# First block column pair of the conv mixer and of the second feed-forward: seven-product scheme against eight plain block products

## The chip, the cores and the metric

One core of one Trainium2 chip runs the whole program in one launch. The metric is the device time of that core in microseconds (us), median of three runs. TensorE multiplies and sums into PSUM, ScalarE, VectorE and GpSimd work between SBUF and PSUM, and SyncE issues every DMA of the part that matters here.

## The reference, cut to what matters

A step of a two-layer decoder trunk: 1024 prompt tokens and 32 sample tokens, 1056 in all, model width 1024, everything in float32. Layer 0 is sparse attention and a feed-forward, layer 1 a short convolution mixer and a feed-forward. Each sub-layer first normalises its input and scales and shifts it by a condition.

```python
hp = rms_norm(yp, norm1_g[i]) * (1.0 + sc1p) + sh1p
bg, cg, hv = jnp.split(h @ w_in, 3, axis=-1)      # conv mixer, w_in 1024 x 3072
u = cg * hv
y = sum(conv_k[j] * up[:, j:j + T] for j in range(CONV_WIDTH))
return (bg * y) @ w_out
g, u = jnp.split(h @ w_gu, 2, axis=-1)            # feed-forward, w_gu 1024 x 5632
return (jax.nn.silu(g) * u) @ w_down
```

## The kernel before, in words

**Precision.** Each float32 operand is split in two parts, high (a rounded copy, made by ScalarE) and low (the difference, made by VectorE or GpSimd). A product of two blocks is three matmuls: high by high, high by low, low by high.

**Layout.** The result `y` lies in SBUF as eight rows of 128 features by 1056 tokens. The tokens are two groups of 528 (`GS`), a group two halves of 264 (`H`). The three phases behind the attention (`ffn0`, `conv`, `ffn1`, numbered f = 0, 1, 2) share one code. A phase is a list of items (`outline`). A "U" item is one kind of weights (conv: c, h, b; feed-forward: g, u) for a pair of 128-wide output columns. "D" items are the product that comes down again, "P" and "Z" the plain rest of it.

**Seven products.** A U item splits weights (two output columns by two halves of the inner dimension) and tokens (two halves of features by two halves of a group) into 2 x 2 blocks, and gets the four result blocks by seven products in place of eight (Strassen's scheme in Winograd's form). The seven are taken in the order `ORD = (1, 2, 6, 5, 7, 3, 4)`. Products 1, 2 and 3 take token blocks as they are. Products 5, 6, 7 and 4 take sums of token blocks. Of the weights, products 6, 5, 3 and 7 take sums too, made by VectorE (`dve_sums`). A group's token operands are the buffer `th[s]`, with a place `T_AT[i]` for the operand of product i. Results are taken out of PSUM piece by piece by ScalarE (`act_take`) and VectorE (`dve_take`), which add partial results; for kind g a Silu comes on top (`act_silu`).

**First pair of a phase.** Its items are run for one group at a time: kind 1 of group 0, kind 2 of group 0, kind 1 of group 1, kind 2 of group 1. All later ones take both groups at once, 168 matmuls an item. One group takes 84: 7 products, 4 steps of the inner dimension, 3 matmuls. Only the first item of a phase waits for its tokens (`fresh`, in `pe_tokens_ready`), step by step.

**Start of a phase.** While Z runs, ScalarE squares the finished rows, GpSimd adds them (`pool_add`), TensorE sums over the features with a matrix of ones (`pe_sum`), VectorE forms mean and reciprocal, ScalarE the root. Then for group 0, feature tile k by feature tile k (0 to 3), VectorE scales two rows (`dve_scaled`), ScalarE applies scale and shift (`act_affine`), VectorE makes four sums (`dve_t123`, `dve_t4`), ScalarE the high parts (`act_high_b`, `act_high_t`), VectorE the low parts (`dve_low`). The same for group 1 is put between the positions of the first two items (`dve_build`, `act_build`). `pe_sum(f, 1)` stands in TensorE's queue ahead of the first item.

**Weights.** A loaded item lies in one of two raw buffers. Its blocks go one by one through a ring of four, high part by ScalarE (`act_split`), low part mostly by GpSimd (`pool_split`), some by VectorE (`dve_split`). Block n + 4 is prepared at the position of block n. Every engine works its queue in the written order; semaphores tie the queues together.

Of the kernel before, what the change touches and what calls it, by code (L numbers as in the profile page):

```python
# [147 lines left out]
T_AT = {4: 0, 5: 1, 6: 2, 7: 3, 1: 4, 2: 5, 3: 6}  # L148
# [15 lines left out]
def outline(name):  # L164

    kinds, pairs = KINDS[name], N_PAIRS[name]
    for j in range(pairs):
        if j == 0 and name == "conv":
            yield from (("U", k, j, 0, (s,)) for s in BOTH for k in "ch")
            yield "U", "b", j, 0, BOTH  # L170
        elif j == 0:
            yield from (("U", k, j, 0, (s,)) for s in BOTH for k in kinds)
        else:
            yield from (("U", k, j, 0, BOTH) for k in kinds)
# [10 lines left out]
for _f, _name in enumerate(PHASES):  # L185
    for _stage, _kind, _at, _e, _groups in outline(_name):
        _n, _k = len(ITEMS), 7 if _stage in "UD" else 4
        ITEMS.append(Item(_n, _f, _stage, _kind, _at, _e, _groups, len(PREP), None if _stage == "Z" else len(RING), _res))
        for _pos in range(_k):
            if _stage != "Z":  # L190
                SLOT[len(PREP)] = len(RING)
                RING.append(len(PREP))
                DONE.append(_res + (_pos + 1 if _stage == "U" else 2 * _pos + 2 if _stage == "D" else 8 + 8 * (_pos // 2)))
            PREP.append((_n, _pos))
        _res += _k if _stage == "U" else 14 if _stage == "D" else 16
N_RES = _res
IN_PHASE = [[it for it in ITEMS if it.phase == f] for f in range(3)]
U_ITEMS = [[it for it in p if it.stage == "U"] for p in IN_PHASE]
# [6 lines left out]
def units_of(it):  # L205
    return 7 if it.stage in "UD" else 16
# [20 lines left out]
def lo_engine(p):  # L227

    it, pos = ITEMS[PREP[p][0]], PREP[p][1]
    if it.stage != "U":  # L230
        return "pool"
    first = IN_PHASE[it.phase][0].prep
    if p < first + 4:
        return "dve" if it.phase else "pool"
    return "dve" if pos in (1, 6) else "pool"
# [27 lines left out]
for _it in ITEMS:  # L263
    for _u in range(units_of(_it)):
        for _q in range(2 if _it.stage == "D" else 1):
            _set = _par + 2 * _q
            _who = "dve"
            if _it.stage == "U":
# [11 lines left out]
        if _it.stage == "U" and _it.kind in "gc":  # L280
# [4 lines left out]
for _it in ITEMS:  # L285
    if _it.stage == "U" and _it.kind in "ub":
        for _s in _it.groups:
            PAIR_END[_it.phase, _it.at, _s] = TAKEN[_it.res + 6]
PIECE_AT, PIECES_END, _tp = {}, {}, 0
for _a, _b in zip(ITEMS, ITEMS[1:]):  # L290
    if _a.stage == "U" and _a.kind in "ub":
# [32 lines left out]
def lop(g, k, i):  # L324
# [4 lines left out]
    return 20 * g + 5 * k + at + 1  # L329


def program(nc, x_prompt, x_sample, c_prompt, c_sample, cache_k, cache_v, cache_kidx, state_conv, page_table,
# [12 lines left out]
    with ExitStack() as ctx:  # L345
# [43 lines left out]
        (nb0,) = place(AREA["half1"] + 8320, ("nb0", [P, 4, 2, GS], F32))  # L389
# [3 lines left out]
        th = (th0, th1)  # L393
        stages = (stage0, stage1)
# [1893 lines left out]
        def sp_raw(sp, n):  # L2288
# [4 lines left out]
            if n >= 2:  # L2293
                done = ITEMS[n - 2].prep + units_of(ITEMS[n - 2]) - 1 if ITEMS[n - 2].stage in "UD" else ITEMS[n - 2].prep + 3
# [4 lines left out]
            for a in range(2):  # L2299
# [5 lines left out]
                if it.stage == "U":  # L2305
# [47 lines left out]
        def sp_phase(sp, f):  # L2353
            chunks = N_CHUNKS[PHASES[f]]
            for it in U_ITEMS[f]:
# [3 lines left out]
                for k in range(7):  # L2359
# [88 lines left out]
        def pe_u_item(pe, it):  # L2448
            fresh = it.at == 0 and it.kind == FIRST_KIND[it.phase]
            for pos, i in enumerate(ORD):  # L2450
# [3 lines left out]
                for s in it.groups:  # L2454
                    out, x = PS[:, 2 * SET[r] + s, 0:H], th[s][:, :, T_AT[i]]
# [75 lines left out]
        def pe_phase(pe, f):  # L2531
            for it in U_ITEMS[f]:
                if f and it is U_ITEMS[f][0]:
                    pe_sum(pe, f, 1)
                pe_u_item(pe, it)
# [29 lines left out]
        def act_piece(act, n, k):  # L2565
# [6 lines left out]
            act.wait_ge(rd_d, PAIR_END[ph, j, 1 if s is None else s])  # L2572
            after(act, t_st[tp % 2], 16 * (tp // 2))
# [50 lines left out]
        def act_u_item(act, it):  # L2624
            for pos in range(7):
                act_piece(act, it.n, pos)
# [3 lines left out]
                if it.at == 0 and it.groups == (0,):  # L2630
                    act_build(act, it.phase, pos + (7 if it.kind in "uh" else 0))

# [47 lines left out]

        def norm_source(f, s, k, i):
# [24 lines left out]
        def act_z(act, f):  # L2706
# [11 lines left out]
            for i in range(3, 6):  # L2718
                act_square(act, g, 1, i)
            act_affine(act, g, 0, 0)  # L2720
            act_high_b(act, g, 0, 0)
            act_square(act, g, 1, 6)
            act_affine(act, g, 0, 1)
            act_square(act, g, 1, 7)
            act_high_t(act, g, 0, 0)
            act_high_b(act, g, 0, 1)
# [732 lines left out]
```

## Time and profile before

| | us |
|---|---|
| median of 3 runs (2718.96 to 2723.64) | 2723.47 |
| profiled execution | 2723.55 |
| its span, first to last instruction | 2721.7 |
| TensorE busy | 2515.4 (92%) |
| VectorE busy | 1866.8 (69%) |
| ScalarE busy | 1156.2 (42%) |
| GpSimd busy | 1298.9 (48%) |
| mean granted TensorE clock | 0.963 |

Times in the rows are counted from the first instruction. The phase `conv` begins where the Z item of `ffn0` ends, at 1552 us, the phase `ffn1` at 1954 us. TensorE's share is a mean: it is near full within a phase and falls at the starts of phases.

### The profile page before, as it was taken

The numbers are of one execution on the slowest core, as the hardware profiler recorded it, in microseconds if no ns is written. First come the engines' busy times: TensorE is split into PE (matmuls) and PEld (weight loads), VectorE is DVE, ScalarE is ACT, GpSimd is POOL, SyncE is SP. The second block draws the span as 40 slices with busy tenths as digits, with TensorE's granted clock in tenths as the row PEclk, the third lists the DMA queues.
The fourth block names the chain that finished last, engine by engine and source line by source line (L and its number), as shares of the span: only waits on it lengthen the run. The fifth ranks groups of instructions, "written<-read, shape, count | busy, mean of one in ns | idle before, by whom it ended". The sixth has DMA issues, their size and how long they took to land.

```text
span 2721.7 us, 51667 instructions
## 1 busy us (share of the span) xinstructions
PE 2515.4 (92%) x19876; PEld 2309.1 (85%) x19876; DVE 1866.8 (69%) x3356; ACT 1156.2 (42%) x2216; POOL 1298.9 (48%) x988
## 2 busy tenths in 40 slices
PE   6979989999977999999999769999779999999999
PEld 4848864677876999999999769999669999999999
DVE  6488888664269665656667797766796657556675
ACT  4156646774245444444222453332364444442223
POOL 3404642442144656656544435445336566565444
PEclk7999999999997999999999979999889999999999
DMA  8305566103332434444974213328224344359741
GB/s 313 85 17 169 172 225 223 39 1 107 101 96 79 151 127 159 134 143 158 360 294 172 92 52 119 103 87 323 84 59 155 121 159 147 120 183 365 284 152 68
DMA packets 316391, 407.99 MB, mean 150 GB/s; under 512 B 40816, under 2 KB 227032, under 8 KB 313338
## 3 DMA queue, kind: packets, MB, share of 16 engines
q1 hardware_dynamic: 316154, 404.75, 44.3%
q8 instruction: 159, 2.61, 0.4%
q14 instruction: 78, 0.64, 0.1%
HBM read 284.85 MB, written 119.85 MB: 149 GB/s over the span
## 4 chain that ended last, share of the span: by engine, by line
PE 67%; DVE 16%; issue 6%; DMA 5%; POOL 3%; ACT 2%; SPq 1%; DVEq 0%; ACTq 0%; POOLq 0%
PE PS L2460 10%; PE PS L2462 10%; PE PS L2461 10%; PE PS L572 9%; PE PS L2482 5%; PE PS L2484 4%; PE PS L2485 4%; PE PS L1818 2%; PE PS L1847 2%; PE PS L1829 2%; DVE th L2783 1%; DVE s_all L1515 1%; DVE tA L2877 1%; DVE y L2881 1%; POOL ring L2755 1%
## 5 line engine op out<-in xcount | busy, mean ns | idle before, releaser
L2460 PE MATMUL PS<-th,ring 128*128 128x264 f32 x3136 | 911.2, 291 | 79.0 <-DVE y L2914 31.7
L2462 PE MATMUL PS<-th,ring 128*128 128x264 f32 x3136 | 903.7, 288 | 0.0
L2461 PE MATMUL PS<-th,ring 128*128 128x264 f32 x3136 | 902.9, 288 | 0.0
L2460 PEld LDWEIGHTS PS<-th,ring 128*128 128x128 f32 x3136 | 602.4, 192 | 93.1 <-issue 79.4
L2461 PEld LDWEIGHTS PS<-th,ring 128*128 128x128 f32 x3136 | 603.0, 192 | 0.3
L2462 PEld LDWEIGHTS PS<-th,ring 128*128 128x128 f32 x3136 | 603.0, 192 | 0.0
L2755 POOL TENSOR_TENSOR ring<-sums,ring 128x512 fp32r<-128x512 f32 x248 | 363.9, 1469 | 339.1 <-ACT ring L2563 338.8
L2755 POOL TENSOR_TENSOR ring<-wraw,ring 128x512 fp32r<-128x512 f32 x215 | 305.7, 1423 | 370.7 <-ACT ring L2563 370.1
L2482 PE MATMUL PS<-th,ring 128*128 128x264 f32 x1232 | 354.5, 288 | 15.0 <-DVE zs L2973 5.1
L2484 PE MATMUL PS<-th,ring 128*128 128x264 f32 x1232 | 353.1, 287 | 0.0
L2485 PE MATMUL PS<-th,ring 128*128 128x264 f32 x1232 | 352.6, 286 | 0.0
L2970 DVE SCALAR_TENSOR_TENSOR y<-PS,mod,y 128x528 f32<-128x528 f32 x308 | 234.8, 766 | 142.8 <-PE PS L2485 129.8
L2563 ACT ACTIVATE ring<-wraw 128x512 fp32r<-128x512 f32 x340 | 212.5, 626 | 277.0 <-PE PS L2485 169.5
L2914 DVE TENSOR_TENSOR y<-y,PS 128x528 f32<-128x528 f32 (+1 forms) x186 | 120.1, 646 | 304.8 <-PE PS L2462 304.4
L2563 ACT ACTIVATE ring<-sums 128x512 fp32r<-128x512 f32 x252 | 158.1, 630 | 394.5 <-PE PS L2462 175.6
L2482 PEld LDWEIGHTS PS<-th,ring 128*128 128x128 f32 x1232 | 234.7, 191 | 16.8 <-issue 11.0
L2485 PEld LDWEIGHTS PS<-th,ring 128*128 128x128 f32 x1232 | 234.8, 191 | 0.0
L2484 PEld LDWEIGHTS PS<-th,ring 128*128 128x128 f32 x1232 | 234.6, 190 | 0.0
L2768 POOL TENSOR_TENSOR stage<-y,stage 128x528 fp32r<-128x528 f32 x110 | 180.7, 1643 | 66.0 <-ACT stage L2581 66.0
L2609 ACT ACTIVATE y<-PS 128x528 f32<-128x528 f32 (+1 forms) x215 | 121.2, 564 | 214.0 <-PE PS L2462 213.7
L572 PE MATMUL PS<-hhi,uhi 128*128 128x352 f32 (+1 forms) x552 | 189.9, 344 | 19.9 <-DVE hlo L1244 7.3
L572 PE MATMUL PS<-hhi,ulo 128*128 128x352 f32 (+1 forms) x552 | 181.2, 328 | 0.0
(393 smaller groups left out, 4702.1 us busy)
## 6 DMA issues: line engine op xcount, KB each, us to landing
t_scratch<-stage SPq DMA_DIRECT2D x154, 528.0 KB, 3.2
th<-t_scratch SPq DMA_DIRECT2D x77, 1056.0 KB, 8.9
wraw<-in_ffn_w_gu_dram SPq DMA_DIRECT2D x96, 512.0 KB, 5.1
wraw<-in_ada_w_dram SPq DMA_DIRECT2D x80, 512.0 KB, 4.6
wraw<-in_ffn_w_down_dram SPq DMA_DIRECT2D x80, 256.0 KB, 6.0
wraw<-in_conv_w_in_dram SPq DMA_DIRECT2D x28, 512.0 KB, 5.1
y<-y_scratch SPq DMA_DIRECT2D x12, 1056.0 KB, 9.3
y_scratch<-y SPq DMA_DIRECT2D x6, 2112.0 KB, 7.8
```

The costliest lines, as they stand in the source:

```text
L572: last = pe.matmul(out, w(kt), x(kt), start=(n == 0), stop=(n == 3 * count - 1))
L2460: pe.matmul(out, hi, x[:, TH, k, :], start=(k == 0 and i in (1, 2, 5)), stop=False, skip_group_check=True)
L2461: pe.matmul(out, hi, x[:, TL, k, :], start=False, stop=False, skip_group_check=True)
L2462: last = pe.matmul(out, lo, x[:, TH, k, :], start=False, stop=(k == 3), skip_group_check=True)
L2482: pe.matmul(out, hi, x[:, TH, 2 * k + s, :], start=(k == 0 and i in (1, 2, 5)), stop=False, skip_group_check=True)
L2484: pe.matmul(out, hi, x[:, TL, 2 * k + s, :], start=False, stop=False, skip_group_check=True)
L2485: last = pe.matmul(out, lo, x[:, TH, 2 * k + s, :], start=False, stop=(k == 1), skip_group_check=True)
L2563: act.activation(slot_of(p)[:, RH, :], split_source(p), ACT.Copy).then_inc(w_hi, 1)
L2609: act.activation(out, result(r, it.groups), ACT.Silu if it.kind == "g" and pos == 6 else ACT.Copy).then_inc(rd_a, 1)
L2755: pool.tensor_tensor(w[:, RL, :], split_source(p), w[:, RH, :].bitcast(F32), ALU.subtract).then_inc(w_lop, 1)
L2768: pool.tensor_tensor(lo.rearrange("p (s n) -> p s n", s=2), token_part(v, i), hi.rearrange("p (s n) -> p s n", s=2), ALU.subtract).then_in ...
L2970: ins = dve.scalar_tensor_tensor(out=out, in0=result(r, BOTH), scalar=gate_of(f, m)[:, 0:1], in1=out, op0=ALU.mult, op1=ALU.add)
```

## The change

For the phases `conv` and `ffn1` the first pair's first two kinds become "C" items, one for each kind and group, with two units of 48 matmuls instead of seven products of 12: 96 matmuls an item. The four plain weight blocks and four plain token blocks are used, and the results of one output column (`mi`) lie ready in two PSUM banks. One take of 528 columns by ScalarE (kinds g and c, Silu included) or by VectorE (u and h, times the other kind) empties both.

`norm_row` now lies in `xf`, inside `th` itself. For each of eight rows `act_row` applies scale and shift and makes the high part, `dve_low_row` the low part. The token sums of a group are made for all four k at once (1056 columns), from step 4 on: `dve_sum_ops`, `act_high_sum`, `dve_low_sum`. The sum for product 7 takes the place of the plain block in the same place of `th`, so that it waits for the group's C items; for group 1 it is made in the next item. `pe_sum(f, 1)` moves behind the first unit. A C item has four weight blocks, none of them a sum.

```diff
-T_AT = {4: 0, 5: 1, 6: 2, 7: 3, 1: 4, 2: 5, 3: 6}
+T_AT = {4: 0, 5: 1, 6: 2, 1: 3, 7: 4, 2: 5, 3: 6}
...
+            yield from (("C", k, j, 0, (s,)) for s in BOTH for k in kinds[:2])
+            yield from (("U", k, j, 0, BOTH) for k in kinds[2:])
...
+        def pe_c_item(pe, it):
...
+            for mi in range(2):
+                r = it.res + mi
+                pe_bank_free(pe, r)
+                for b in range(2):
...
+                    pe_split_ready(pe, p)
+                    for k in range(4):
+                        if fresh and mi == 0:
+                            pe.wait_ge(n_lop, row_lo(f, s, 4 * b + k))
...
+                        for h in range(2):
...
+                            pe.matmul(out, hi, x[:, TH, k, :], start=(b == 0 and k == 0), stop=False, skip_group_check=True)
+                            pe.matmul(out, hi, x[:, TL, k, :], start=False, stop=False, skip_group_check=True)
+                            last = pe.matmul(out, lo, x[:, TH, k, :], start=False, stop=(b == 1 and k == 3), skip_group_check=True)
+                last.then_inc(r_mm, 1)
+                if fresh and s == 0 and mi == 0:
+                    pe_sum(pe, f, 1)
...
+        def dve_c_build(dve, f, step):
...
+            if step == 1:
+                dve_mean(dve, f, 1)
+                dve_recip(dve, f, 1, 0)
+                dve_recip(dve, f, 1, 1)
+                dve_samples(dve, f)
+                dve_row(dve, f, 1, 0)
+                dve_row(dve, f, 1, 1)
+            if step == 2:
+                for ft in range(4):
+                    dve_low_row(dve, f, 1, ft)
+                    dve_row(dve, f, 1, ft + 2)
+            if step == 3:
+                for ft in range(4, 8):
+                    dve_low_row(dve, f, 1, ft)
+                    if ft < 6:
+                        dve_row(dve, f, 1, ft + 2)
+            if step > 3 and step % 2 == 0:
+                s = step // 2 - 2
+                dve_sum_ops(dve, f, s, 5)
+                dve_sum_ops(dve, f, s, 6)
+                dve_sum_ops(dve, f, s, 7)
+                dve_low_sum(dve, f, s, 6)
+            if step > 3 and step % 2:
+                s = step // 2 - 2
+                dve_sum_ops(dve, f, s, 4)
+                dve_low_sum(dve, f, s, 5)
+                dve_low_sum(dve, f, s, 4)
+                if s == 0:
+                    dve_low_sum(dve, f, s, 7)
...
+        def act_c_item(act, it):
+
+            step = 2 * (it.kind in "uh") + 4 * it.groups[0]
+            for mi in range(2):
+                act_c_build(act, it.phase, step + mi)
+                act_c_take(act, it, mi)
+                for pos in (2 * mi, 2 * mi + 1):
+                    act_split(act, PREP_AT[it.n, pos])
...
             dve_recip(dve, g, 0, 1)
+            dve_row(dve, g, 0, 0)
+            dve_row(dve, g, 0, 1)
             dve_plain(dve, it, 13)
-            dve_scaled(dve, g, 0, 0)
-            dve_plain(dve, it, 14)
...
+            for ft in range(8):
+                if ft < 6:
+                    dve_row(dve, g, 0, ft + 2)
+                if ft in (1, 3):
+                    dve_plain(dve, it, 14 if ft == 1 else 15)
+                dve_low_row(dve, g, 0, ft)
+                if ft == 4:
+                    dve_fix(dve, g)
             dve_reduce(dve, g)
```

## Rows read from the trace of the kernel before

**Rows 1.** The page's busy times by engine, with shares of the span.
```profile
PE 2515.4 (92%) x19876; PEld 2309.1 (85%) x19876; DVE 1866.8 (69%) x3356; ACT 1156.2 (42%) x2216; POOL 1298.9 (48%) x988
```
**Rows 2.** TensorE's waits: waiting line, releaser, us in total, times, longest.
```profile
PE PS L2460 <- DVE y L2914: 31.7, 39, 4.3
PE PS L2460 <- issue: 31.0, 12, 7.1
PE PS L2528 <- issue: 29.2, 2, 14.6
```
**Rows 3.** Windows: length, busy us (count) by engine, granted clock, DMA share, GB/s.
```profile
1552.40:1568.80 16.40, 1.83 (x8) 1.32 (x6) 16.19 (x35) 11.37 (x24) 3.57 (x3) 0.65 0.36 132
1568.80:1596.70 27.90, 15.67 (x87) 14.45 (x85) 27.70 (x56) 15.00 (x33) 5.90 (x4) 0.78 0.14 39
1596.70:1618.50 21.80, 16.07 (x84) 15.18 (x85) 21.29 (x46) 14.60 (x32) 7.38 (x5) 0.69 0.12 34
1618.50:1640.60 22.10, 21.13 (x168) 20.59 (x169) 16.70 (x23) 10.96 (x22) 13.95 (x11) 1.00 0.40 108
...
1970.40:2019.80 49.40, 30.24 (x170) 28.07 (x169) 48.96 (x101) 31.98 (x69) 12.97 (x9) 0.79 0.13 37
```
**Rows 4.** Timeline of TensorE, at the edges of items: start, us, engine, line.
```profile
1552.40 0.29 PE L2516 MATMUL PS<-za,zw 128*128 128x280 f32 x1
1567.27 2.10 PE L2528 MATMUL PS<-accs,ones 128*128 128x264 f32 x4 [14.57 <-issue]
...
1640.60 0.36 PE L2460 MATMUL PS<-th,ring 128*128 128x264 f32 x1 [0.65 <-DVE y L2914]
...
1650.50 0.36 PE L2460 MATMUL PS<-th,ring 128*128 128x264 f32 x1 [0.90 <-DVE y L2914]
...
2052.55 0.36 PE L2460 MATMUL PS<-th,ring 128*128 128x264 f32 x1 [1.63 <-DVE y L2914]
```
**Rows 5.** Timeline of TensorE: neighbours at the lower and at the full level.
```profile
1569.60 0.42 PE L2462 MATMUL PS<-th,ring 128*128 128x264 f32 x1
1569.82 0.42 PE L2460 MATMUL PS<-th,ring 128*128 128x264 f32 x1
...
1618.70 0.29 PE L2461 MATMUL PS<-th,ring 128*128 128x264 f32 x1
1618.82 0.28 PE L2462 MATMUL PS<-th,ring 128*128 128x264 f32 x1
```
**Rows 6.** Timeline of VectorE: the forms the walk is made of.
```profile
1562.13 0.70 DVE L3060 TENSOR_TENSOR nb<-y,rs 128x528 f32<-128x528 f32 x1
1562.75 0.43 DVE L3071 TENSOR_TENSOR t<-nb 128x264 f32<-128x264 f32 x1
...
1576.61 1.79 DVE L3034 RECIPROCAL rs<-rs 128x264 f32<-128x264 f32 x1
...
1647.73 1.28 DVE L2946 SCALAR_TENSOR_TENSOR y<-y,vec_g 128x1024 f32<-128x1024 f32 x1
```
**Rows 7.** Timeline of ScalarE: rows of group 0, and a table load.
```profile
1551.56 1.55 ACT L2669 ACTIVATE nb<-nb,mod,gsc 128x528 f32<-128x528 f32 x2
...
1553.47 0.63 ACT L2678 ACTIVATE th<-nb 128x528 fp32r<-128x528 f32 x1
...
1983.19 1.28 ACT L2622 ACT_TABLE_LOAD   x1
```
**Rows 8.** Timeline of VectorE and GpSimd together.
```profile
1600.88 1.29 DVE L3059 COPY tB<-zs 128x32 f32<-128x32 f32 x1
...
1602.67 0.17 DVE L3059 COPY tB<-zs 128x32 f32<-128x32 f32 x1
...
1600.32 1.81 POOL L2755 TENSOR_TENSOR ring<-sums,ring 128x512 fp32r<-128x512 f32 x1 [4.68 <-ACT ring L2563]
```
**Rows 9.** Timeline within the Z item of ffn0: VectorE, then TensorE.
```profile
1525.92 1.80 DVE L2833 TENSOR_TENSOR ring<-wraw,ring 128x512 fp32r<-128x512 f32 x1
...
1528.55 0.36 PE L2514 MATMUL PS<-za,zw 128*128 128x264 f32 x1 [1.76 <-DVE y L3007]
```

More of the change, by code:

```diff
@@ L167, in outline @@
     for j in range(pairs):
-        if j == 0 and name == "conv":
-            yield from (("U", k, j, 0, (s,)) for s in BOTH for k in "ch")
-            yield "U", "b", j, 0, BOTH
+        if j == 0 and name == "ffn0":
+            yield from (("U", k, j, 0, (s,)) for s in BOTH for k in kinds)
         elif j == 0:
-            yield from (("U", k, j, 0, (s,)) for s in BOTH for k in kinds)
+            yield from (("C", k, j, 0, (s,)) for s in BOTH for k in kinds[:2])
+            yield from (("U", k, j, 0, BOTH) for k in kinds[2:])
         else:
@@ L278 @@
         _par ^= 1
[L280 removed]
+        if _it.stage in "CU" and _it.kind in "gc":
             _gated = _count["act"]
@@ L329, in lop, with row_lo, sum_lo, sum_op @@
     return 20 * g + 5 * k + at + 1
+T_ORD = (6, 5, 4, 7)
+def row_lo(f, s, ft):
+    return 40 + 24 * (f - 1) + 8 * s + ft + 1
+def sum_lo(f, s, i):
+    return 40 + 24 * (f - 1) + 16 + 4 * s + T_ORD.index(i) + 1
+def sum_op(f, s):
+    return 32 + 8 * (f - 1) + 4 * s
+C_END = {(it.phase, it.groups[0]): it.res + 2 for it in ITEMS if it.stage == "C"}
 def program(nc, x_prompt, x_sample, c_prompt, c_sample, cache_k, cache_v, cache_kidx, state_conv, page_table,
@@ L2625, in act_u_item @@
             for pos in range(7):
+                if pos == 0 and it.phase and ITEMS[it.n - 1].stage == "C":
+                    act_high_sum(act, it.phase, 1, 7)
                 act_piece(act, it.n, pos)
@@ L2791, in pool_u_item @@
         def pool_u_item(pool, it):
-            for pos in range(7):
+            for pos in range(4 if it.stage == "C" else 7):
                 pool_piece(pool, it.n, pos)
                 pool_split(pool, PREP_AT[it.n, pos])
-                if it.at == 0 and it.groups == (0,):
+                if it.phase == 0 and it.at == 0 and it.groups == (0,):
                     pool_build(pool, it.phase, pos + (7 if it.kind in "uh" else 0))
@@ L2960, in dve_u_item, with dve_c_take @@
                     dve_build(dve, it.phase, pos + (7 if it.kind in "uh" else 0))
+                late = p
+            return late
+        def dve_c_take(dve, it, mi):
+            if it.kind not in "uh":
+                return
+            r, s = it.res + mi, it.groups[0]
+            dve.wait_ge(rd_a, TAKEN[ITEMS[it.n - 1].res + mi])
+            dve.wait_ge(r_mm, r + 1)
+            row = 1 + 2 * mi if it.kind == "h" else v_row(it.phase, 0) + mi
+            halves = lambda a: y[:, a, group(s)].rearrange("p (h n) -> p h n", h=2)
+            dve.tensor_tensor(halves(row), PS[:, 2 * SET[r]:2 * SET[r] + 2, 0:H], halves(4 + mi), ALU.mult).then_inc(rd_d, 1)
@@ L2961, in dve_u_item, with dve_c_item @@
+        def dve_c_item(dve, it, late):
+            step = 2 * (it.kind in "uh") + 4 * it.groups[0]
+            for pos in range(4):
+                p = PREP_AT[it.n, pos]
+                dve_split(dve, late)
+                if pos % 2 == 0:
+                    dve_c_build(dve, it.phase, step + pos // 2)
+                else:
+                    dve_c_take(dve, it, pos // 2)
+                dve_sums(dve, p + 1)
                 late = p
```

177 lines of the change are left out of this document (120 added, 57 removed).

## The prediction

> **What bounds the kernel now.** I read the page first: TensorE is busy for 92% of the span [rows 1], so what can be won without fewer matmuls lies in its gaps. The waits name them [rows 2]: U matmuls behind VectorE's takes 31.7 us, behind nothing the profile can name ("issue": the wait for several semaphores at once) 31.0 us in 12 places, and `pe_sum` 29.2 us in 2 places. The two are the starts of `conv` and `ffn1`. Windows there [rows 3] show the exchange: from 1552.4 to 1568.8 TensorE is busy 1.8 of 16.4 us and VectorE 16.2; in the first item, 1568.8 to 1596.7, 15.7 of 27.9 against 27.7; in the second, 16.1 of 21.8 against 21.3. In items 3 and 4, TensorE is busy 21.1 of 22.1 us. So at the start of a phase VectorE is the bound, for 66 us, and `ffn1` repeats it (30.2 against 49.0 of 49.4). The seven products want the four token sums of all tiles before the first item can go on, and TensorE's granted clock is 0.65 to 0.79 in these windows.
>
> Fixed points [rows 4]: Z's last matmul starts at 1552.4, `pe_sum` at 1567.3, the first item of both groups ("b") at 1640.6, its fourth position at 1650.5. With 24 matmuls a position and 0.122 us from one to the next at the full level, 2.4 GHz (0.12 between neighbours [rows 5], and 168 in 20.5 us), b's seventh position starts at 1650.5 + 3 x 2.93 = 1659.3. `ffn1` is the same 401.6 us later: its fourth position is at 2052.55, so its seventh at 2061.3, or 1659.7 in `conv`'s time.
>
> **The change, part by part.**
> *More matmuls.* Four items of 96 for 84: 48 more a phase, 5.9 us at 0.122, 11.7 us in both. They lie on TensorE, but in time in which it waits now.
>
> *Group 0's rows.* For two rows VectorE now issues 12 operations (2 scalings, 4 sums, 6 low parts, most of them of 264 columns); in the change it is one scaling and one low part of 528 columns a row, 0.62 us each from start to start (1562.13 to 1562.75 [rows 6]). ScalarE needs for a row 0.80 (two in 1.55, and the copy must wait for its own result) and 0.52 (0.63 by its end, the next 0.1 earlier) [rows 7]: 1.35 us. Two plain takes of Z, `dve_fix`, three squares and the samples' square lie between. Two scaled rows are now ahead of take 13, which holds Z's last product back 1.3 us; ScalarE's first row then comes at 1552.9 instead of 1551.6. Eight rows at 1.35 are 10.8, two squares between them 1.1, two holds by GpSimd's adds 1.8, the last row's low part behind it 1.3: 1567.9 or so. TensorE starts its first matmul at 1555.1 instead of 1568.8, and goes along row by row, six matmuls each (1.3 us at the lower level, 0.73 at the full one), up to 1567.9; `pe_sum` follows (0.8), then the second unit (5.9): 1574.5. The second item's 96 matmuls end at 1586.2.
>
> *Group 1's rows, all sums: does VectorE keep up?* From 1567.7 its queue holds, up to its last take of the fourth item: mean 0.6, two reciprocals 3.5 (1.79 by its end, 1.72 from start to start [rows 6]), samples 1.2, eight rows of 0.66 with the small copy 5.3, eight low parts 5.0, four takes 2.5, and 15 operations of 1056 columns (8 sums, 7 low parts). The trace has none of these. Lower end: 0.62, the price of 528 columns; upper end: four operations of 264, 0.43 each in a dependent run, 1.7 [rows 6]. I take 1.16: 264 more columns cost 0.27, and 1024 columns in another form take 1.28 by their end. 15 x 1.16 = 17.4. Weight sums of b 1.2, its one block 0.6. Together 37.3 us.
>
> To this comes GpSimd. While its low part of a weight block runs, VectorE's operations out of SBUF stand still: a copy of 32 columns takes 1.29 us when GpSimd began before it, 0.17 otherwise, and it ends as GpSimd's does [rows 8]: 1.1 us lost. 14 such blocks lie in this stretch, 12 of which meet a queued operation: 13 us. Waits for ScalarE's high parts add 3.7. So VectorE reaches the last take at 1567.7 + 37.3 + 13 + 3.7, about 1621.8. The Trainium skill, "SBUF — State Buffer", section "Who interferes with whom", says that a Vector instruction with two SBUF inputs and a GpSimd instruction that reads SBUF exclude each other for the whole instruction. By that rule it is 13 us a phase, as the row has it; were bandwidth shared, it would be near none.
>
> Walking the four queues in their order with these prices gives TensorE's starts in `conv`: third item 1587.8 (1.6 late, VectorE's take of the second item stands behind its rows), fourth 1602.4 (2.6 late, its weights' high parts stand behind ScalarE's high sums, which wait for VectorE), b 1615.9 (1.8 late), b's second position 1621.9 (3.1 late, it waits for the take just placed), the seventh 1640.1, with one more wait behind the conv taps. Gain: 1659.3 - 1640.1 = 19.2 us. In `ffn1` Silu and Sqrt alternate now: two more table loads of 1.28 [rows 7] stand ahead of the root and move the chain by 2.2 us. Behind b's place stands the token work of the pair, with the high sum for product 7 ahead of it on ScalarE. Seventh position at 1642.2: gain 17.5.
>
> *Weights.* 12 blocks and 16 weight sums fewer a phase. In Z, VectorE does without three sums (0.6 to 1.4 us each); it stood 1.80 us on one low part, and TensorE waited 1.76 us for the take behind these [rows 9]. GpSimd's adds, and so the mean, are as late as the takes. I take 1.3 us a phase (bounds 0 and 1.8). ScalarE's 12 splits fewer are hidden.
>
> *Clock.* At the lower level, 1.2 GHz, it is 0.22 us from matmul to matmul [rows 5]. In the second item now, with a pause at nearly every position, TensorE is busy 16.1 us for 84 matmuls, 10.2 at the full level: 5.9 us by the clock (0.69 [rows 3]), over some four pauses, about 1.5 each. In the walk TensorE pauses so at the second unit (slack behind it) and at b's second position. I charge 1.6 us a phase (bounds 0 and 4).
>
> *At nothing:* loads (the same bytes; a raw buffer is free earlier), the changed places in `th` (same transfers), `ffn0`.
>
> Sum: 19.2 + 17.5 + 2.6 - 3.3 = 36.0 us. The profiled execution took 2723.55 us, 0.1 above the median; 2723.5 - 36 = 2687.5.
>
> **The rivals.**
> *1. All engines keep up* (chance 0.10). Without GpSimd's exclusion the same walk has b at 1608.4 and its seventh position at 1626.0: 33 us a phase, with the other terms 2655. For it: GpSimd is busy only 13 of 49 us there in `ffn1` now [rows 3]. Against it: rows 8, and that VectorE has no free microsecond now.
>
> *2. A new wait takes most of it* (0.12). The sums cost 1.6 us instead of 1.16: then the walk's gain is 12.5 and 10.8, with the other terms 2701; or VectorE's lateness runs on into the items behind b, where now it is even with TensorE (16.7 of 22.1 us busy in items 3 and 4 [rows 3], so that it has caught up by b). Each item more in which it is late costs some 3 us, the wait seen at b's second position: five of them, 2702. Both, 2716.
>
> *3. Slower: the clock* (0.05). C items are fed row by row and with small pauses; in 1596.7 to 1618.5 a like rhythm gave a granted clock of 0.69 [rows 3]. If TensorE stays at 1.2 GHz through the C items, a unit takes 10.6 us instead of 5.9: 1568.7 for the second unit, six more units behind it, 7 x 10.6 = 74, b at 1644.1 with small waits, its seventh position at 1663.9 and 1665.0. That is 4.6 + 5.3 = 10 us lost, 2.6 won at Z, 2731. It decides from about 0.20 us a matmul on. Against it: a unit has 48 matmuls with no wait inside, and items 3 and 4, runs of 84, had the full level (1.00 [rows 3]). The Trainium skill, "TensorE: Matmul & The Clock Gate", section on the clock gate, has the level follow how busy the array has been; by it the row-paced first unit could stay low, which costs nothing, and the rest rise.
>
> *4. The sums are dearer than thought* (0.02, slower or the same): at 2.4 us each the gain is gone. Nothing in rows 6 speaks for it.
>
> **How the numbers follow.** Forecast 0.71 (its own range 2674 to 2699), rivals 0.10, 0.12, 0.05, 0.02. The range that leaves two in ten out: from 2668, part of the way to rival 1 (sums at 0.62 would give 26.1 + 24.4, 2674), to 2708, into rival 2. A measurement here tells 0.2%, 5.4 us, from no change. Faster by more: 0.71 + 0.10 + 0.11 = 0.92; within 0.02; slower 0.06.
>
> **What would show it.** TensorE's first C matmul some 1.4 us behind Z's last, at the pace of ScalarE's rows (1.3 to 1.6 us for six). No wait of 14.6 us ahead of `pe_sum`. VectorE busy or held from there to b's second position, the wide operations at 1.2 us, up to 2.3 where GpSimd runs. b about 62 us behind Z's last matmul (88 now), and a wait of 3 us ahead of b's second position. Wrong if b comes later than 80 us, if matmuls of C items follow each other at 0.22 beyond the second unit, or if waits grow in items behind b that are smooth now.

## The result, and the profile after

The changed kernel takes 2678.84 us (median of 4 runs, 2675.16 to 2681.85) against 2722.02 for the kernel before on the same chip: ratio 0.9842 [0.9825, 0.9859], 43 us or 1.6% faster. In two later comparisons, both on one chip, the same kernel, run as a control, gave 0.9832 [0.982, 0.9845] and 0.9863 [0.9846, 0.988].

The page's busy times, which answer to [rows 1]: 96 matmuls more for TensorE, but 47 us less work for VectorE and a span 41.6 us shorter (2680.1 us).
```profile
PE 2518.1 (94%) x19972; PEld 2313.5 (86%) x19972; DVE 1819.6 (68%) x3182; ACT 1137.3 (42%) x2120; POOL 1294.9 (48%) x978
```
TensorE's waits, against [rows 2]: the 29.2 us ahead of `pe_sum` are gone, "issue" ahead of U matmuls (L2493 now) fell from 31.0 to 17.9, the takes from 31.7 to 15.1. New are the waits of C matmuls (L2517): 4.8 us behind Z's takes, 4.7 behind GpSimd's low parts, 4.4 behind VectorE's low parts of the rows, 1.9 behind a take, 15.8 in all; and b's second position behind the last take of the C items (L3078), twice 3.1 us.
```profile
PE PS L2493 <- issue: 17.9, 5, 7.1
PE PS L2493 <- DVE y L3017: 15.1, 29, 3.6
PE PS L2571 <- DVE zs L3215: 6.3, 4, 2.2
PE PS L2493 <- DVE y L3078: 6.2, 2, 3.1
PE PS L2517 <- DVE zs L3215: 4.8, 2, 2.4
PE PS L2517 <- POOL ring L2858: 4.7, 4, 2.1
PE PS L2517 <- DVE th L3094: 4.4, 4, 1.2
```
Windows of `conv` (columns as in [rows 3]): Z's last matmul to the first C matmul; the first unit; `pe_sum` and the second unit; the second item; the third item; b. The fourth item's row stands in the last section. The last row here is the item behind b in `ffn1`, where "b" stands for the phase's first item of both groups (kind g of its second pair). In the 13.8 us behind Z's last matmul (first two rows) TensorE is busy 9.2 us, where it was busy 1.8 of 16.4, and it is busy all the time in the next two rows. VectorE is busy for 54.7 of the 60.7 us up to b, most of the time, as forecast. The granted clock is 0.69 in the row-paced first unit and 1.00 in the next three rows; it is 0.87 in the fourth item and 0.89 in b.
```profile
1552.20:1554.90 2.70, 0.29 (x3) 0.06 (x1) 2.10 (x5) 2.64 (x4) 0.50 (x1) 1.00 0.00 0
1554.90:1566.00 11.10, 8.89 (x47) 8.05 (x48) 10.45 (x16) 8.90 (x14) 2.52 (x2) 0.69 0.22 79
1566.00:1572.90 6.90, 6.90 (x55) 6.77 (x54) 4.87 (x5) 2.28 (x4) 2.54 (x2) 1.00 1.04 299
1572.90:1584.70 11.80, 11.80 (x98) 11.64 (x96) 10.28 (x20) 10.13 (x16) 5.65 (x4) 1.00 0.44 116
1584.70:1599.50 14.80, 12.52 (x97) 11.90 (x96) 13.70 (x15) 9.46 (x15) 5.58 (x5) 1.00 0.26 71
...
1612.90:1643.30 30.40, 23.51 (x171) 23.15 (x170) 27.62 (x42) 8.38 (x13) 10.23 (x6) 0.89 0.13 36
...
2021.30:2045.50 24.20, 22.27 (x171) 22.08 (x170) 9.35 (x11) 7.37 (x13) 8.81 (x7) 0.93 0.35 112
```
TensorE's timeline at the edges, against [rows 4]: first C matmul, b's second and fourth position in `conv`, and a wait in the item behind `ffn1`'s b. b itself starts at 1612.91 (1640.6 before), its seventh position at 1640.37 (1659.35).
```profile
1554.92 0.39 PE L2517 MATMUL PS<-th,ring 128*128 128x264 f32 x1 [2.43 <-DVE zs L3215]
...
1619.13 0.36 PE L2493 MATMUL PS<-th,ring 128*128 128x264 f32 x1 [3.10 <-DVE y L3078]
...
1629.02 0.56 PE L2493 MATMUL PS<-th,ring 128*128 128x264 f32 x1 [3.80 <-issue]
...
2026.32 0.36 PE L2493 MATMUL PS<-th,ring 128*128 128x264 f32 x1 [1.94 <-ACT y L2666]
```
VectorE's wide sums in `conv`, and GpSimd beside them: 1.25 us alone, 2.33 inside GpSimd's run.
```profile
1594.51 1.25 DVE L3111 TENSOR_TENSOR rs<-xf 128x1056 f32<-128x1056 f32 x1
...
1600.46 2.33 DVE L3121 TENSOR_TENSOR th<-tB,th 128x1056 fp32r<-128x1056 f32 x1
...
1597.97 5.96 POOL L2858 TENSOR_TENSOR ring<-wraw,ring 128x512 fp32r<-128x512 f32 x3 [4.50 <-ACT ring L2618]
```
The profiled executions, cut at marks on TensorE, say where the time came from (us; Z first and last are its matmuls, "ninth" is the ninth item behind b):

| stretch | conv before | conv after | gain | ffn1 before | ffn1 after | gain |
|---|---|---|---|---|---|---|
| Z first to Z last | 31.62 | 29.47 | 2.2 | 31.53 | 28.19 | 3.3 |
| Z last to b's seventh position | 106.95 | 88.17 | 18.8 | 107.39 | 87.53 | 19.9 |
| from there to the ninth item | 171.36 | 171.19 | 0.2 | 169.19 | 172.76 | -3.6 |

That is 40.8 us of the 41.7 between the profiled executions. There is one trace of the kernel before; in the two controls, the stretches of the changed kernel are the same to 1.7 us (Z 29.5 and 29.9 in `conv`, 28.4 and 28.2 in `ffn1`).

### The profile page after: what moved, and what is told of

Read it like the earlier page. It is cut to its first block, busy times and chain, and to the rows that moved or that the text cites. A ratio compares the mean times of both kernels' runs of the same rounds, so it can differ in the third digit from the quotient of the medians.

```text
span 2680.1 us, 51467 instructions
## 1 busy us (share of the span) xinstructions
PE 2518.1 (94%) x19972; PEld 2313.5 (86%) x19972; DVE 1819.6 (68%) x3182; ACT 1137.3 (42%) x2120; POOL 1294.9 (48%) x978
## 4 chain that ended last, share of the span: by engine, by line
PE 66%; DVE 15%; DMA 6%; issue 5%; POOL 4%; ACT 2%; SPq 2%; DVEq 0%; ACTq 0%; POOLq 0%
PE PS L2493 10%; PE PS L2495 9%; PE PS L2494 9%; PE PS L602 9%; PE PS L2539 4%; PE PS L2541 4%; PE PS L2542 4%; PE PS L1848 3%; PE PS L1877 3%; PE PS L1859 2%; DMA a_scratch<-stage 1%; DVE s_all L1545 1%; DVE y L2984 1%; DVE tA L2980 1%; POOL ring L2858 1%
## 5 line engine op out<-in xcount | busy, mean ns | idle before, releaser
L2493 PE MATMUL PS<-th,ring 128*128 128x264 f32 x2912 | 841.3, 289 | 49.8 <-issue 17.9
L2495 PE MATMUL PS<-th,ring 128*128 128x264 f32 x2912 | 835.7, 287 | 0.0
L2494 PE MATMUL PS<-th,ring 128*128 128x264 f32 x2912 | 835.1, 287 | 0.0
L2493 PEld LDWEIGHTS PS<-th,ring 128*128 128x128 f32 x2912 | 556.3, 191 | 59.4 <-issue 53.3
L2494 PEld LDWEIGHTS PS<-th,ring 128*128 128x128 f32 x2912 | 556.8, 191 | 0.1
L2495 PEld LDWEIGHTS PS<-th,ring 128*128 128x128 f32 x2912 | 556.6, 191 | 0.0
L2858 POOL TENSOR_TENSOR ring<-wraw,ring 128x512 fp32r<-128x512 f32 x225 | 327.4, 1458 | 357.8 <-ACT ring L2618 356.8
L2858 POOL TENSOR_TENSOR ring<-sums,ring 128x512 fp32r<-128x512 f32 x228 | 337.3, 1481 | 302.3 <-ACT ring L2618 302.2
L2539 PE MATMUL PS<-th,ring 128*128 128x264 f32 x1232 | 353.3, 287 | 14.9 <-POOL ring L2858 5.0
L2541 PE MATMUL PS<-th,ring 128*128 128x264 f32 x1232 | 351.8, 286 | 0.0
L2542 PE MATMUL PS<-th,ring 128*128 128x264 f32 x1232 | 351.4, 285 | 0.0
L3017 DVE TENSOR_TENSOR y<-y,PS 128x528 f32<-128x528 f32 (+1 forms) x162 | 109.9, 678 | 303.0 <-PE PS L2495 302.9
L2618 ACT ACTIVATE ring<-sums 128x512 fp32r<-128x512 f32 x228 | 143.2, 630 | 370.1 <-PE PS L2495 180.1
L2539 PEld LDWEIGHTS PS<-th,ring 128*128 128x128 f32 x1232 | 233.3, 189 | 16.8 <-issue 11.1
L2542 PEld LDWEIGHTS PS<-th,ring 128*128 128x128 f32 x1232 | 233.6, 190 | 0.0
L2541 PEld LDWEIGHTS PS<-th,ring 128*128 128x128 f32 x1232 | 233.3, 189 | 0.0
L2666 ACT ACTIVATE y<-PS 128x528 f32<-128x528 f32 (+1 forms) x187 | 110.5, 591 | 195.2 <-PE PS L2495 193.7
## 6 DMA issues: line engine op xcount, KB each, us to landing
wraw<-in_ffn_w_gu_dram SPq DMA_DIRECT2D x96, 512.0 KB, 5.3
wraw<-in_ada_w_dram SPq DMA_DIRECT2D x80, 512.0 KB, 4.7
wraw<-in_conv_w_in_dram SPq DMA_DIRECT2D x28, 512.0 KB, 5.3
```

What stands on the lines that cost most here:

```text
L2493: pe.matmul(out, hi, x[:, TH, k, :], start=(k == 0 and i in (1, 2, 5)), stop=False, skip_group_check=True)
L2494: pe.matmul(out, hi, x[:, TL, k, :], start=False, stop=False, skip_group_check=True)
L2495: last = pe.matmul(out, lo, x[:, TH, k, :], start=False, stop=(k == 3), skip_group_check=True)
L2539: pe.matmul(out, hi, x[:, TH, 2 * k + s, :], start=(k == 0 and i in (1, 2, 5)), stop=False, skip_group_check=True)
L2541: pe.matmul(out, hi, x[:, TL, 2 * k + s, :], start=False, stop=False, skip_group_check=True)
L2542: last = pe.matmul(out, lo, x[:, TH, 2 * k + s, :], start=False, stop=(k == 1), skip_group_check=True)
```

## The experiments

Times and ratios are against the kernel before on the same chip. Differences of a few us drown in the spread of whole runs (3 to 15 us within a kernel, part of it from ahead of `conv`), so I also give the stretch from Z's last matmul to the ninth item, summed over both phases: 554.9 us before; 519.7, 518.4 and 518.5 in three executions of the changed kernel. 518.9 is their mean. Every other kernel has one profiled execution, so a difference of under 2 us from it is none, and one of 3 or 4 us is weak.

| kernel | median | ratio | interval | stretch | against 518.9 |
|---|---|---|---|---|---|
| e1_sum_first | 2693.52 | 0.9906 | 0.9891 to 0.9921 | 533.2 | +14.3 |
| e2_short_pool | 2650.27 | 0.9749 | 0.9736 to 0.9762 | 494.2 | -24.7 |
| e3_low_on_vector | 2673.17 | 0.9829 | 0.9814 to 0.9845 | 510.7 | -8.2 |
| e4_84_matmuls | 2673.90 | 0.9827 | 0.9813 to 0.9841 | 516.1 | -2.8 |
| control | 2675.40 | 0.9832 | 0.9820 to 0.9845 | 518.4 | |
| e5_take_first | 2674.34 | 0.9827 | 0.9807 to 0.9847 | 518.1 | -0.8 |
| e6_sum_and_root_first | 2685.70 | 0.9881 | 0.9864 to 0.9898 | 526.6 | +7.7 |
| e7_both | 2676.22 | 0.9832 | 0.9817 to 0.9847 | 514.7 | -4.2 |
| e8_rows_first | 2694.83 | 0.9917 | 0.9901 to 0.9932 | 536.1 | +17.2 |
| e9_taps_behind | 2674.85 | 0.9842 | 0.9828 to 0.9856 | 515.4 | -3.5 |
| e10_three | 2674.12 | 0.9844 | 0.9828 to 0.9860 | 512.0 | -6.9 |
| control2 | 2679.86 | 0.9863 | 0.9846 to 0.9880 | 518.5 | |

### e1_sum_first: what the early first unit is worth

```diff
+                if f and it is U_ITEMS[f][0]:
+                    pe_sum(pe, f, 1)
                 (pe_c_item if it.stage == "C" else pe_u_item)(pe, it)
...
-                if fresh and s == 0 and mi == 0:
-                    pe_sum(pe, f, 1)
```


> The changed kernel with pe_sum(f, 1) put back ahead of the phase's first item, so that TensorE can't begin on group 0's rows while they are made. Theory (VectorE's queue, held by GpSimd, bounds the start of a phase up to b's second position): TensorE runs its first unit after the sum, 6 to 7 us late, but has 4.8 us of waits to give in the third and fourth C item; what is left is VectorE's takes of the second item coming about 2 us late. 3 to 5 us slower than the changed kernel over both phases. Rival (the gain is TensorE's early start, its stream is the bound): a whole unit and its lower clock level is lost in each phase, 12 to 15 us slower.

It costs 14.3 us by the stretches: the theory's small price fell. The first C matmul starts 14.8 us behind Z's last (2.7 in the changed kernel). ScalarE and VectorE in `conv` show how this reaches the engine that sets the pace:
```profile
1572.08 0.61 ACT L2701 ACTIVATE y<-PS 128x528 f32<-128x528 f32 x1 [9.45 <-PE PS L2519]
1572.59 1.14 ACT L2618 ACTIVATE ring<-wraw 128x512 fp32r<-128x512 f32 x2
1573.63 0.63 ACT L2750 ACTIVATE rs<-rs 128x528 f32<-128x528 f32 x1
...
1574.30 3.46 DVE L3239 RECIPROCAL rs<-rs 128x264 f32<-128x264 f32 x2 [7.79 <-ACT rs L2750]
```
ScalarE's root of group 1 stands behind its take of the first unit. The take waits 9.45 us for TensorE, and VectorE 7.79 us for the root. By TensorE's units alone b would start 14.8 + 8 x 5.9 = 62 us behind Z's last, 1.3 later than in the changed kernel (60.7); it starts at 68.1. In `ffn1` the same sum gives 62.4 us, earlier than the changed kernel's 63.6. So TensorE's early unit isn't only work done in idle time; it also lets ScalarE's queue go on. How much of the 14.3 us goes this way, e1 alone can't tell; e6 and e8 try it.

### e2_short_pool: what GpSimd's runs cost VectorE

GpSimd makes the low parts of the C items' weight blocks for 32 of 512 columns; the low parts of the other columns are left out.
```diff
+            q = ITEMS[PREP[p][0]]
+            n = 32 if q.stage == "C" or (q.stage == "U" and q.phase and ITEMS[q.n - 1].stage == "C") else 512
-            pool.tensor_tensor(w[:, RL, :], split_source(p), w[:, RH, :].bitcast(F32), ALU.subtract).then_inc(w_lop, 1)
+            pool.tensor_tensor(w[:, RL, 0:n], split_source(p)[:, 0:n], w[:, RH, 0:n].bitcast(F32), ALU.subtract).then_inc(w_lop, 1)
```


> The changed kernel with GpSimd's low parts of the C items' weight blocks, and of the item behind them, made for 32 of 512 columns only; the rest of these low parts is left out. Theory: GpSimd no longer holds VectorE, some 12 holds of 1.1 us a phase are gone, 20 to 26 us faster than the changed kernel. Rival (both engines share the way to SBUF without stopping each other, or TensorE is the bound): only the weights come earlier, 0 to 6 us faster.

24.7 us less, 13.4 and 12.1 in the two phases against the changed kernel's own profile. In `conv`, 8.2 us of it are there at b's second position, the rest comes within b, whose blocks were shortened too. VectorE's wide sums in `conv`, third item:
```profile
1585.27 1.26 DVE L3123 TENSOR_TENSOR th<-tA,th 128x1056 fp32r<-128x1056 f32 x1
1586.44 1.31 DVE L3123 TENSOR_TENSOR th<-tB,th 128x1056 fp32r<-128x1056 f32 x1
1587.68 1.25 DVE L3123 TENSOR_TENSOR th<-rs,th 128x1056 fp32r<-128x1056 f32 x1
```
These three took 2.14, 2.33 and 2.33 us in the changed kernel. Of its 32 wide operations in both phases, 18 take 1.25 or 1.26 us, two 1.7 and twelve 2.14 to 2.35; in e2 all 32 take 1.24 to 1.33. So the holds are shown by a run. Their size isn't quite the forecast's 13 us a phase: from Z's last matmul to b's second position VectorE's operations are together 9.3 us shorter in e2 in `conv` and 10.1 in `ffn1`, by 11 and 12 operations. That the weights come earlier is in e2's gain as well, but the expectation's rival gave this 0 to 6 us in all. The Trainium skill, "SBUF — State Buffer", section "Who interferes with whom", has a VectorE instruction with two SBUF inputs and a GpSimd instruction that reads SBUF lock each other out; the rows agree, held operations being up to 1.1 us longer.

### e3_low_on_vector: the same parts by VectorE itself

```diff
     if it.stage == "C":
-        return "pool"
+        return "dve"
```


> The changed kernel with the low parts of the C items' weight blocks made by VectorE (0.61 us each) instead of GpSimd: 12 blocks a phase more on VectorE. Theory: each took 1.1 us from VectorE by its hold and takes 0.6 now, 4 to 8 us faster over both phases, less where VectorE now stands waiting for ScalarE's high part. Rival (what counts is VectorE's own work, 7.3 us more a phase, and GpSimd's holds fall into its pauses): 8 to 15 us slower.

The stretches are 8.2 us shorter. VectorE takes on 0.6 us a block and is spared a hold of up to 1.1. The median, 0.9829 beside 0.9832 and 0.9863 of the controls, can't show it; its profiled execution came to `conv` 7 us later than the control's, in code that no edit touches.

### e4_84_matmuls: the added matmuls

High by low only for k = 0 of the second block; the other products of that kind are left out.
```diff
+                            if b == 0 or k == 0:
-                            pe.matmul(out, hi, x[:, TL, k, :], start=False, stop=False, skip_group_check=True)
+                                pe.matmul(out, hi, x[:, TL, k, :], start=False, stop=False, skip_group_check=True)
```


> The changed kernel with 12 of the 96 matmuls of each C item left out (the high by low product of the second inner half, for three of four k): 84, as many as the seven products had. It prices the extra matmuls. Theory: TensorE waits for VectorE at the third item, the fourth, b and b's second position, so 48 matmuls fewer a phase bring 0 to 3 us over both phases. Rival (TensorE's stream is the bound): 48 x 0.122 = 5.9 us a phase, 9 to 12 us faster.

2.8 us less for 96 matmuls fewer, 11.7 us at 0.122, and even these can't be put to the matmuls. Up to b's seventh position the two phases add up to 175.0 us, and to 175.7, 174.3 and 174.7 in the three executions of the changed kernel: nothing. The 2.8 us lie behind it, where no matmul was left out. So all 96 lie in time in which TensorE would wait.

### control, e5_take_first: the wait ahead of b's second position

The control is the changed kernel unaltered. e5 puts VectorE's last take of the fourth C item ahead of the last sums.
```diff
-                else:
+                elif step + pos // 2 != 7:
                     dve_c_take(dve, it, pos // 2)
...
+                    if step + pos // 2 == 7:
+                        dve_c_take(dve, it, 1)
                     dve_c_build(dve, it.phase, step + pos // 2)
```


> The changed kernel again, unaltered, beside the others of this call: 2675 to 2680 us, some 43 us under the kernel before.

> The changed kernel with VectorE's last take of the fourth C item ahead of the three wide operations of step 7, so that the wait of 3.1 us ahead of b's second position goes. Theory: VectorE has the same work and is the bound up to b's fourth position; the wait moves there: 0 to 3 us faster over both phases. Rival (the wait is a matter of order alone): 3.1 us a phase, 6 us faster.

Nothing to be measured, and TensorE's timeline in `conv` says why: the second position comes early, and the fourth waits 6.25 us instead of 3.8.
```profile
1614.12 0.37 PE L2493 MATMUL PS<-th,ring 128*128 128x264 f32 x1 [1.25 <-POOL ring L2858]
...
1623.55 0.56 PE L2493 MATMUL PS<-th,ring 128*128 128x264 f32 x1 [6.25 <-issue]
```

### e6_sum_and_root_first: is it the root alone?

e1's edit, and ScalarE's root at step 0, ahead of its first take.
```diff
-            if step == 1:
+            if step == 0:
                 act_root(act, f, 1)
```


> As e1_sum_first (pe_sum ahead of the first C item), and group 1's root moved ahead of ScalarE's take of the first unit, behind which it stood: in e1 VectorE waited 7.8 us for that root, so e1 had delayed VectorE's chain as well as TensorE. Theory (VectorE's queue is the bound, TensorE's early unit is worth only what it lets VectorE's chain begin): of e1's 13.5 us most comes back, 3 to 6 us slower than the changed kernel over both phases. Rival (TensorE's stream itself): still 12 to 14 us slower.

+7.7 us, half of e1's price and above the 3 to 6 expected. The wait moved one step down the same queue (ScalarE, then VectorE, `conv`):
```profile
1575.22 0.61 ACT L2701 ACTIVATE y<-PS 128x528 f32<-128x528 f32 x1 [4.19 <-PE PS L2519]
1575.73 1.14 ACT L2618 ACTIVATE ring<-wraw 128x512 fp32r<-128x512 f32 x2
1576.77 0.79 ACT L2779 ACTIVATE xf<-xf,mod,gsc 128x496 f32<-128x496 f32 x1
...
1578.27 1.27 DVE L3094 TENSOR_TENSOR th<-xf,th 128x528 fp32r<-128x528 f32 x1 [7.66 <-ACT th L2783]
```
ScalarE's first row of group 1 stands behind its take of the second unit.

### e7_both

e3 and e5 together.

> e3_low_on_vector (low parts of the C items' weights by VectorE) and e5_take_first together. Theory: e3's gain in the two phases by its trace, 8 to 9 us, of which the run's median showed 3 beside a start 2 us late, and up to 3 by the order: 8 to 12 us faster than the changed kernel. Rival (one takes the other's gain): no more than e3 alone, 3 to 9 us.

4.2 us by the stretches, half of what was expected and less than e3 alone (8.2), and nothing in the median. In `conv` most of what it is behind e3 comes at b's fourth position: its 24 matmuls take 5.41 us behind the wait, 2.99 in e3. b's second position came 4.4 us earlier in `conv` than in the control, its fourth by 0.6: the wait there grew to 6.27 us, as in e5. In the control VectorE (first two rows) and TensorE stand so:
```profile
1623.15 0.69 DVE L2963 TENSOR_TENSOR sums<-wraw,sums 128x512 f32<-128x512 f32 x1
1623.76 0.69 DVE L3017 TENSOR_TENSOR y<-y,PS 128x528 f32<-128x528 f32 x1
...
1624.55 0.56 PE L2493 MATMUL PS<-th,ring 128*128 128x264 f32 x1 [3.79 <-issue]
```
Ahead of the first row lie the first conv taps, from 1617.8 to 1623.1. TensorE starts when the take L3017 has ended.

### e8_rows_first: root and rows ahead

e6's edit, and rows 0 to 3 of group 1 on ScalarE at step 0, on VectorE at step 1.
```diff
-            if step == 1:
+            if step == 0:
                 act_root(act, f, 1)
-            if step in (2, 3):
+                for ft in range(4):
+                    act_row(act, f, 1, ft)
+            if step == 3:
```


> The token sum of group 1 again ahead of the first C item, ScalarE's root and now also its first four rows of group 1 ahead of its take of the first unit (VectorE's part of these rows moved with them). With the root alone moved the two phases took 4.4 and 3.9 us longer than in the changed kernel, and VectorE stood 7.66 us for ScalarE's first row of group 1, which came behind ScalarE's take of the second unit at 1575.2. Theory: an order in ScalarE's queue is all that ties the build of group 1 to TensorE's late stream. Then with the rows ahead VectorE's wait goes below 2 us, and what is left is TensorE's own bound: first C matmul 13 to 15 us behind Z's last, eight units of 5.9 us from there, b at 61 to 64 us behind Z's last (60.6 in the changed kernel), b's seventh position 0 to 3 us later than in the changed kernel: 0 to 5 us in all over the control. Rival: the late start of the stream itself costs, through the weight ring or the clock; then the phases stay 4 us longer each, 8 us in all.

My theory's number fell: +17.2 us, worse than e1. VectorE's wait of 7.66 us did go (0.88 for the first row), but ScalarE, VectorE's rows being ready only at 1572.1, now makes the high parts of the second item's weights behind the rows, and GpSimd its low parts behind these (ScalarE, GpSimd, TensorE):
```profile
1577.78 0.59 ACT L2701 ACTIVATE y<-PS 128x528 f32<-128x528 f32 x1
1578.27 1.14 ACT L2618 ACTIVATE ring<-wraw 128x512 fp32r<-128x512 f32 x2
...
1578.96 5.15 POOL L2860 TENSOR_TENSOR ring<-wraw,ring 128x512 fp32r<-128x512 f32 x4 [19.87 <-ACT ring L2618]
...
1580.55 0.56 PE L2517 MATMUL PS<-th,ring 128*128 128x264 f32 x1 [3.36 <-POOL ring L2860]
```
So root, rows and weights all share ScalarE's queue with takes that wait for TensorE; of the three orders tried with a late stream none is free. Whether a finer mix would be was not tried. That ScalarE's order is the cause is shown for about half of e1's price, by e6, the only one that got some of it back; for the rest it is argued from the waits, and the late start of the stream itself, through the weight ring, is not ruled out.

### e9_taps_behind, e10_three, control2

e9 puts b's first taps behind the take of its second product and behind the weight sum; e10 is e9 with e3 and e5.
```diff
-                if it.kind == "b" and pos in (0, 2):
+                behind = it.kind == "b" and it.at == 0
+                if it.kind == "b" and pos in (0, 2) and not (behind and pos == 0):
                     dve_taps(dve, it, pos // 2)
-                dve_take(dve, it, pos)
+                dve_take(dve, it, pos, behind and pos == 1)
...
             dve.tensor_tensor(out, out, result(r, it.groups), ALU.add).then_inc(rd_d, 1)
+            if taps:
+                dve_taps(dve, it, 0)
             if it.kind in "uhb":
```


> In b of the first pair the first three-tap convolution on VectorE (5.3 us from 1617.8 to 1623.1) comes behind the weight sum and the take of b's second product, which stood behind it, and not ahead. TensorE waits 3.8 us ahead of b's fourth position in the changed kernel until that take has emptied a bank. Theory: the wait goes, and b's seventh position in conv comes 3 to 5 us earlier; ffn1 has no taps and doesn't move. In all 3 to 5 us. Rival: VectorE has the same work in b and is the bound there up to the sixth position; then a wait of 2 to 4 us appears one or two positions later, and 0 to 1 us is left.

> Three edits together: VectorE makes the low parts of the C items' weight blocks in place of GpSimd, the last take of the fourth C item stands ahead of the last sums, and b's first taps stand behind the take of its second product. The first two together moved b's second position up by 4.4 us and its fourth by only 0.6, because TensorE waited 6.3 us there for the take behind the taps. Theory: with the taps moved both gains stay: b's seventh position in conv 5 to 9 us earlier than in the control, in ffn1 3 us as with the first two, 8 to 12 us in all, beyond both kernels. Rival: VectorE is behind in b in any order; then conv gives 0 to 2 us, ffn1 3, 3 to 5 us in all, hardly to be told from the control.

> The changed kernel unaltered, for comparison on the same chip: 2672 to 2680 us, two phases (from Z's last matmul to the tenth item) of 259 to 260 us each.

e9: no wait of 2 us or more is left ahead of the fourth position, and one of 2.24 us appears ahead of the seventh, behind VectorE's low part. b's seventh position is 85.3 us behind Z's last (88.2, 88.1 and 86.7 in the three executions of the changed kernel): some 2 us less than their mean, between theory and rival, and the 3.5 of the stretches has a spread of 1.3 to set against it. e10, TensorE's two waits in b behind its third position and the operation that ends the second:
```profile
1617.94 0.36 PE L2493 MATMUL PS<-th,ring 128*128 128x264 f32 x1 [1.98 <-issue]
...
1630.81 0.38 PE L2493 MATMUL PS<-th,ring 128*128 128x264 f32 x1 [3.86 <-DVE ring L2936]
...
1629.40 0.69 DVE L2936 TENSOR_TENSOR ring<-wraw,ring 128x512 fp32r<-128x512 f32 x1
```
The fourth position comes 71.6 us behind Z's last, 5 us earlier than in the control, the seventh 84.5: VectorE, without a pause from 1610 to 1635, gives out there instead. 6.9 us by the stretches, less than the 8 to 12 of the theory, and no better than e3 alone (8.2): that the three edits add up is not shown. The medians of e9 and e10 lie 5 and 6 us under control2, and all five runs of e9 (2672.3 to 2676.1) lie under its four (2677.3 to 2681.5), but the intervals touch and the first control had 2675.4: that either beats the changed kernel is likely by the trace and not shown by the times.

## Why the prediction was right

The forecast of 2687.5 us, 36.0 gained, stands against 43 (and 37 and 46 in the controls, from their ratios): 8.7 us high, the sign, the mechanism and most places right. Of the 8.7, 1.5 are the kernel before, whose median is now 2722.0. (In the forecast's sum, two phases at 1.6 for the clock are 3.2, not 3.3.)

The forecast had put into its walk that Z's last product comes 1.3 us later. Counted from Z's last matmul, like the table above, it has: Z 0 (1.3 won, 1.3 held back), `conv` 18.9, `ffn1` 17.3, nothing behind. Measured: Z 5.5 in both phases together, 18.8, 19.9, -3.4 behind, 0.9 elsewhere.

- **VectorE's queue with GpSimd's holds** is what sets b's place. The forecast's 37.3 + 13 + 3.7 = 54.0 us, up to VectorE's last take of the fourth item, took 51.7 (1567.25 to 1618.98). The term of the holds was too large: 13 us, for 12 holds of 1.1, against 9.3 by e2. Waits for ScalarE came to 3.1, so that its own work was some 39. Wide operations were taken at 1.16, and start 1.18 us apart; held ones at up to 2.3, and took 2.33. b came 60.7 us behind Z's last matmul (forecast 62), the wait ahead of its second position was 3.10 (3.1). Rival 1 is settled: the holds are there, and without them the kernel is at 2650.3, where its walk gave 2655.
- **The walk**, Z's last matmul to b's seventh position. `conv`: 18.9 forecast, 18.8 measured, and this closely by luck. b's second position came 66.9 us behind Z's last matmul, 1.3 earlier than forecast; from there to the seventh it took 21.3 us, 1.5 longer. The first C matmul came 2.7 us behind Z's last, not 1.4: it needs the bank that VectorE's take at 1554.0 empties, and this take stands behind the low part of row 0. `ffn1`: 17.3 forecast, 19.9 measured, but 3.6 given back in the items behind b.
- **The give-back** is a thing the forecast hadn't placed. ScalarE in `ffn1` waits for the transfer of a token piece out of its buffer, and the take behind it holds TensorE (the wait at 2026.32 above):
```profile
2025.03 0.64 ACT L2638 ACTIVATE stage<-y 128x528 fp32r<-128x528 f32 x1 [4.68 <-DMA t_scratch<-stage]
2025.58 0.59 ACT L2666 ACTIVATE y<-PS 128x528 f32<-128x528 f32 x1
```
  The longest such wait in this place before was 2.84 us. TensorE's waits behind ScalarE's takes are 2.2 us here, 0.4 before. The other half of the 3.6 is the clock: the same matmuls are busy for 169.5 us, 167.8 before, and in e3, with the same wait but 168.0 us busy, 2.2 us are given back. No run takes the transfer away, so its weight is argued from these rows.
- **Z** gave 2.2 and 3.3 us, 5.5 in all where the forecast had 0 at the same marks, and this is the term sized worst. Both of its parts are in the traces: TensorE's timeline in `ffn1`'s Z before, and ahead of Z's last product in `conv` after.
```profile
1930.26 0.36 PE L2514 MATMUL PS<-za,zw 128*128 128x264 f32 x1 [1.76 <-DVE y L3007]
1935.19 0.39 PE L2514 MATMUL PS<-za,zw 128*128 128x264 f32 x1 [1.77 <-DVE y L3007]
...
1550.76 0.38 PE L2571 MATMUL PS<-za,zw 128*128 128x248 f32 x1 [2.17 <-DVE zs L3215]
```
  The last product is held back as forecast: its wait grew from 0.63 to 2.17 us. But the waits for VectorE's takes earlier in Z are gone altogether, 2.2 us in `conv` (1.76 and 0.44) and 3.5 in `ffn1`, and some 1.5 us a phase come by the clock, 0.95 over Z before and 1.00 after. That the gone weight sums are the reason is argued from VectorE's order; no run isolates it.
- **The clock** was charged 1.6 us a phase. In `conv` b's fourth position, 24 matmuls behind a pause of 3.80 us, takes 5.41 us instead of 2.93, and the fourth item's first unit 7.46 instead of 5.84, so 4.1 us. Rival 3 is out: behind the first unit, C units run at 1.00 in three windows and at 0.87 in the fourth.
- **More matmuls at nothing**: e4 gives nothing back for all 96 up to b's seventh position.
- **Rival 2**, a new wait: one mechanism it named, lateness beyond b, is there with 3.6 us, against the 14 or so that it would have taken.

What the forecast left out is that the early start of TensorE feeds ScalarE's queue. It had put the moved `pe_sum` to TensorE's account only; e1 prices that one line at 14 us of the 43, where TensorE's own lateness explains 1.3 in `conv` and nothing in `ffn1`. Moving the root gave about half of it back (e6); how the rest is shared is open.

## What to carry to other kernels

Where an engine's written queue mixes takes of results with the preparation of later operands, a late producer delays the preparation too; look at what stands behind each take before a start is moved. A wait removed ahead of one position is worth only what the next queue entry leaves (e5, e7, e10): read which operation of the bound engine comes next and move that as well. Count a second engine's reads as lost time for VectorE when VectorE is the bound: 0.9 us on the mean and up to 1.1 for each such meeting here, so the cheaper engine on paper may be the dearer one (e3, by one trace).

## What was unexpected of the hardware

A pause doesn't have one price in clock. Windows of the changed kernel: `conv`'s fourth item, b's first position with the wait behind it, and its second position; then the same three in `ffn1`.
```profile
1599.50:1612.90 13.40, 13.34 (x96) 13.37 (x97) 13.26 (x9) 5.64 (x8) 7.99 (x4) 0.87 0.30 79
1612.90:1619.10 6.20, 3.13 (x26) 2.92 (x25) 6.06 (x8) 3.10 (x5) 1.55 (x1) 1.00 0.00 0
1619.10:1622.10 3.00, 2.97 (x24) 3.00 (x25) 3.00 (x2) 1.24 (x2) 3.00 (x3) 1.00 0.02 5
...
1981.20:1994.40 13.20, 12.00 (x96) 11.80 (x96) 13.06 (x9) 5.58 (x8) 7.91 (x4) 1.00 0.30 80
1994.40:2000.70 6.30, 3.19 (x24) 2.98 (x24) 6.16 (x8) 3.10 (x4) 1.54 (x2) 0.93 0.00 0
2000.70:2006.10 5.40, 5.34 (x24) 5.37 (x25) 5.30 (x5) 2.08 (x4) 3.48 (x3) 0.50 0.01 3
```
Behind a wait of 3.10 us each, the same 24 matmuls run at the full level in `conv` and at the lower one in `ffn1`, 2.4 us dearer, though `ffn1`'s fourth item had the higher clock of the two. The Trainium skill, "TensorE: Matmul & The Clock Gate", section on the clock gate, has the level follow how busy the array has been; these two pairs alone don't show that, and no run here was made to test it. Nor is it fixed by the code: in the controls, behind the same wait of 3.1 us, these 24 matmuls take 3.02 and 4.52 us in `conv` and 5.42 and 4.50 in `ffn1`. My 1.5 us a pause was a mean of prices between 0 and 2.5.
